# Two half-token weight units behind each of the second block's norms, in a two-block transformer kernel on one core

## The reference

```
def second_block(x, c, ...):
    x = layer_norm_2(x, emb_ln_g, emb_ln_b)
    ...
        h = x * (1.0 + sc1) + sh1
        p = h @ w_in[l]
        y_a = gmlp_spatial_gating(p[..., :MIX_A], p[..., MIX_A:2 * MIX_A], ...)
        y_b = rwkv7_time_mix(p[..., 2 * MIX_A:], ...)
        mix = jnp.concatenate([y_a, y_b], axis=-1) @ w_out[l]
        x = layer_norm_2(ALPHA * x + gt1 * mix, ln1_g[l], ln1_b[l])
        h = x * (1.0 + sc2) + sh2
        gu = h @ w_ffn_in[l]
        f = (jax.nn.silu(gu[..., :FFN_HIDDEN]) * gu[..., FFN_HIDDEN:]) @ w_ffn_out[l]
        x = layer_norm_2(ALPHA * x + gt2 * f, ln2_g[l], ln2_b[l])
```

## Time and profile before

| what | value |
|---|---|
| median of 3 executions | 1663.46 us (1661.16 to 1664.08) |
| the profiled execution's own time | 1662.28 us |
| its span in the profile | 1660.5 us |
| PE busy | 1576.3 us, 95% of the span |
| DVE, ACT, POOL busy | 995.2, 722.5, 190.9 us |
| mean granted clock of TensorE | 0.988 of full |

### The profile page before, as it was taken

The page is one execution under the profiler, slowest core; times in us unless marked ns, Lnnn a source line. Parts: engine busy times, 40 slices in busy tenths (PEclk is TensorE's granted clock), DMA queues, the critical chain, the costliest instruction groups (busy, mean ns, idle before and its releaser), DMA issues. The chain is left out here.

```text
span 1660.5 us, 24142 instructions
## 1 busy us (share of the span) xinstructions
PE 1576.3 (95%) x9852; PEld 1254.0 (76%) x9852; DVE 995.2 (60%) x1676; ACT 722.5 (44%) x1159; POOL 190.9 (11%) x159
## 2 busy tenths in 40 slices
PE   6999999999999999899999898988998999999997
PEld 5877776788788767676788687767766887888886
DVE  4999985556555476657444647776547353334445
ACT  6543367245523476557622535554424322223112
POOL 2443465400010000000005000000000000000000
PEclk9999999999999999999999999999998999999999
DMA  5232243654464322232334232200012332323331
GB/s 208 93 97 77 78 152 103 204 155 138 136 191 154 114 90 89 67 99 77 114 102 135 70 115 76 77 28 4 4 39 66 113 115 89 101 91 100 90 100 51
DMA packets 45645, 166.07 MB, mean 100 GB/s; under 512 B 5264, under 2 KB 5392, under 8 KB 45536
## 3 DMA queue, kind: packets, MB, share of 16 engines
q1 hardware_dynamic: 42912, 155.95, 29.6%
q0 software_dynamic: 2624, 8.59, 1.8%
HBM read 162.42 MB, written 2.10 MB: 99 GB/s over the span
## 5 line engine op out<-in xcount | busy, mean ns | idle before, releaser
L569 PE MATMUL bank<-h_T_hi,weight_hi 128*128 128x512 f32 x1208 | 488.2, 404 | 8.4 <-DVE conv_in L2102 3.2
L604 ACT ACTIVATE weight_hi<-raw 128x1024 fp32r<-128x1024 f32 x241 | 254.7, 1057 | 549.4 <-PE bank L571 541.0
L612 DVE TENSOR_TENSOR weight_lo<-raw,weight_hi 128x1024 fp32r<-128x1024 f32 x184 | 225.6, 1226 | 432.6 <-ACT weight_hi L604 432.6
L571 PE MATMUL bank<-h_T_hi,weight_lo 128*128 128x512 f32 x1208 | 477.2, 395 | 0.0
L570 PE MATMUL bank<-h_T_lo,weight_hi 128*128 128x512 f32 x1208 | 476.5, 394 | 0.0
L569 PEld LDWEIGHTS bank<-h_T_hi,weight_hi 128*128 128x128 f32 x1208 | 229.5, 190 | 65.8 <-issue 9.9
L570 PEld LDWEIGHTS bank<-h_T_lo,weight_hi 128*128 128x128 f32 x1208 | 229.3, 190 | 51.7 <-issue 3.9
L571 PEld LDWEIGHTS bank<-h_T_hi,weight_lo 128*128 128x128 f32 x1208 | 228.7, 189 | 50.0
L2105 DVE SCALAR_TENSOR_TENSOR bank<-conv_in,columns,bank 128x512 f32<-128x512 f32 x240 | 181.4, 756 | 8.3
L612 POOL TENSOR_TENSOR weight_lo<-raw,weight_hi 128x1024 fp32r<-128x1024 f32 x57 | 139.5, 2448 | 182.6 <-ACT weight_hi L604 182.6
L570 PE MATMUL bank<-branch_lo,weight_hi 128*128 128x512 f32 x192 | 75.5, 393 | 0.0
(11 more groups left out here) (448 smaller groups left out, 2266.5 us busy)
## 6 DMA issues: line engine op xcount, KB each, us to landing
raw<-in_weights SPq DMA_DIRECT2D x289, 512.0 KB, 3.5
x_in<-in_x SPq DMA_DIRECT2D x4, 512.0 KB, 5.5
x_rows<-in_x POOLq DMA_DIRECT2D x4, 512.0 KB, 4.9
out<-x_rows SPq DMA_DIRECT2D x4, 512.0 KB, 2.6
mem_in<-in_mem POOLq DMA_DIRECT2D x2, 512.0 KB, 8.0
ln_rows<-in_ln_g POOLq DMA_DIRECT2D x4, 256.0 KB, 4.1
ln_rows<-in_ln_b POOLq DMA_DIRECT2D x4, 256.0 KB, 4.7
silu_row<-in_c POOLq DMA_DIRECT2D x1, 512.0 KB, 11.1
```

The source lines that it names most:

```text
L569: pe.matmul(o, lhs[0], rhs[0], start=start, stop=False)
L571: return pe.matmul(o, lhs[1], rhs[0], start=False, stop=stop)
L604: act.activation(parts[n % SPLIT][0][:, :], raw[u % RAW][:, :], ACT.Copy).then_inc(*weight_hi.up(u))
L612: engine.tensor_tensor(lo[:, :], raw[u % RAW][:, :], view(hi[:, :]), ALU.subtract).then_inc(*ready.up(u))
```

## The change

The four units ("pu", 0), ("pu", 1), ("ffn_g", 0) and ("ffn_u", 0), called `EARLY`, leave the ring of three places and get hi and lo places of their own: two in the region of y_T, which the end of the first block frees, two in a region of the rwkv stage's work tiles. ACT and DVE split them behind the last unit of w_out (or w_out_2), ahead of the first row's statistics. The units that follow them take their turn in the ring of three: one is split on ACT behind the sixth piece of group 0, two behind all pieces of group 1; DVE makes all three lo parts behind all pieces.

On PE the two units run together, and in halves of the tokens: group 0's tokens with features 0 to 3 of both units, then the transposes of group 1, then group 0's tokens with features 4 to 7, then group 1's tokens with all eight. So 96 matmuls of 128x256 stand for 48 of 128x512 at each of the two places, and both results are ready at the end.

```diff
+EARLY = (("pu", 0), ("pu", 1), ("ffn_g", 0), ("ffn_u", 0))
...
-    turn_of = {u: n for n, u in enumerate(weights_of)}
+    in_turn = [u for u in weights_of if plan[u][0] not in EARLY]
+    turn_of = {u: n for n, u in enumerate(in_turn)}
...
+    here, there = Map(nc, Y_AT, H_AT), Map(nc, B_AT, M_AT)
+    early_parts = {label: (here if n < 2 else there).pair(f"early_weight{n}", [P, UNIT]) for n, label in enumerate(EARLY)}
...
-            if n >= SPLIT:
-                act.wait_ge(*given_back(weights_of[n - SPLIT]))
-            act.activation(parts[n % SPLIT][0][:, :], raw[u % RAW][:, :], ACT.Copy).then_inc(*weight_hi.up(u))
+            if plan[u][0] == EARLY[0]:
+                act.wait_ge(*y_lo.at(KT - 1))
+            elif plan[u][0] == EARLY[2]:
+                act.wait_ge(*yb_lo.at(FW - 1))
+            elif plan[u][0] not in EARLY and turn_of[u] >= SPLIT:
+                act.wait_ge(*given_back(in_turn[turn_of[u] - SPLIT]))
+            act.activation(weight_parts(u)[0][:, :], raw[u % RAW][:, :], ACT.Copy).then_inc(*weight_hi.up(u))
...
+    def first_units(pe, what, labels, rhs):
+
+
+        use = [(unit_bank(pe, label), weight_parts(index[label])) for label in labels]
+        for label in labels:
+            pe.wait_ge(*lo_ready(index[label]))
+
+        def products(g, features):
+            tokens = turned_columns(g)
+            for k in features:
+                pe.wait_ge(*turned_lo.at(what, g, k))
+                for label, (bank, (hi, lo)) in zip(labels, use):
+                    done = mm3(pe, bank[:, tokens], (hi[:, cut(k)], lo[:, cut(k)]), (rhs[0][:, k, tokens], rhs[1][:, k, tokens]),
+                               k == 0, k == KT - 1)
+                    if g and k == KT - 1:
+                        done.then_inc(*product.up(*label))
+
+        products(0, range(KT // 2))
+        pe_turn_group(pe, what, x_rows, 1)
+        products(0, range(KT // 2, KT))
+        products(1, range(KT))
+
...
     def pe_second_in(pe):
-        pe_turn_group(pe, "emb", x_rows, 1)
-        for n in range(4):
-            feature_unit(pe, ("pu", n), unit_bank(pe, ("pu", n)), h2_T,
-                         ready=(lambda k: turned_lo.at("emb", 1, k)) if n == 0 else None)
+        first_units(pe, "emb", EARLY[0:2], h2_T)
+        for n in range(2, 4):
+            feature_unit(pe, ("pu", n), unit_bank(pe, ("pu", n)), h2_T)
...
     def act_first_out(act):
         act_y_hi(act, KT - 1)
-        feed_hi(act, KT - SPLIT)
+        feed_hi(act, KT - SPLIT + 2)
...
             if t == 2:
                 act_modulated(act, what, hi, n, 0, range(6))
+                feed_hi(act)
         act_modulated(act, what, hi, n, 0, range(6, KT))
-        feed_hi(act)
-        act_modulated(act, what, hi, n, 1, range(KT // 2 + 1))
-        feed_hi(act)
-        act_modulated(act, what, hi, n, 1, range(KT // 2 + 1, KT))
-        feed_hi(act)
+        act_modulated(act, what, hi, n, 1, range(KT))
+        feed_hi(act, 2)
...
-        feed_lo(dve, KT // 2 - SPLIT)
+        feed_lo(dve, KT // 2 - SPLIT + 2)
         dve_rows(dve, "emb", h2_T, lambda t: residual(t, 1))
```

More of the change, by code:

```diff
@@ L592, in given_back, with weight_parts @@
         return product.at(*label)
+    def weight_parts(u):
+        return early_parts[plan[u][0]] if plan[u][0] in EARLY else parts[turn_of[u] % SPLIT]
     def feed_hi(act, count=1):
@@ L609, in split_lo @@
     def split_lo(engine, u, ready):
-        hi, lo = parts[turn_of[u] % SPLIT]
+        hi, lo = weight_parts(u)
         engine.wait_ge(*weight_hi.at(u))
@@ L1455, in pe_ffn @@
     def pe_ffn(pe):
-        pe_turn_group(pe, "ln1", x_rows, 1)
-        for n in range(FT):
+        first_units(pe, "ln1", EARLY[2:4], h3_T)
+        for n in range(1, FT):
             if n == 10:
                 pe_gate_rows(pe, 5)
-            feature_unit(pe, ("ffn_g", n), unit_bank(pe, ("ffn_g", n)), h3_T,
-                         ready=(lambda k: turned_lo.at("ln1", 1, k)) if n == 0 else None)
+            feature_unit(pe, ("ffn_g", n), unit_bank(pe, ("ffn_g", n)), h3_T)
             feature_unit(pe, ("ffn_u", n), unit_bank(pe, ("ffn_u", n)), h3_T)
@@ L1926, in act_second_in @@
         for n in range(4):
-            feed_hi(act)
+            if n >= 2:
+                feed_hi(act)
             act_take(act, ("pu", n), u_T[:, n, :], ACT.Gelu_apprx_tanh)
@@ L2072, in act_second_out @@
     def act_second_out(act):
-        feed_hi(act, KT - SPLIT - len(OUT_FEEDS))
+        feed_hi(act, KT - SPLIT - len(OUT_FEEDS) + 2)
     def last_spots(t):
@@ L2082, in act_ffn @@
         for n in range(FT):
-            feed_hi(act)
+            if n:
+                feed_hi(act)
             gate = act_ring.take(act, ("ffn", n), hidden_lo, n)
             act_take(act, ("ffn_g", n), gate, ACT.Silu)
-            feed_hi(act)
+            if n:
+                feed_hi(act)
             act.wait_ge(*taken["dve"].at("ffn_u", n))
@@ L2537, in dve_rows @@
             dve_modulated(dve, what, pair, 0, k)
-        feed_lo(dve)
         for k in range(KT):
             dve_modulated(dve, what, pair, 1, k)
-            if k in (KT // 2, KT - 1):
-                feed_lo(dve)
+        feed_lo(dve, 3)
     def dve_gain_rows(dve, what, t, half, gains):
@@ L2553, in dve_second_in @@
         for n in range(4):
-            feed_lo(dve)
+            if n >= 2:
+                feed_lo(dve)
             for half in range(2):
```

## The result

| | before | changed |
|---|---|---|
| median, executions beside each other | 1663.77 us (1661.16 to 1664.38, 4) | 1652.90 us (1652.38 to 1653.91, 4) |
| the same text once more (e11 below) | 1663.03 us (17) | 1654.58 us (6) |
| the profiled execution, its span | 1662.28, 1660.5 us | 1653.91, 1652.2 us |

The ratio is 0.9936 with a 95% interval of 0.9922 to 0.9950, and 0.9954 (0.9940 to 0.9968) in the repeat: 8.5 to 10.9 us by the medians, 8.4 between the two profiled executions. The prediction was 1655.3 us, faster, with a range of 1652.0 to 1659.4.

What follows compares the result with a forecast made beforehand. PE was taken as the bound, busy 95% of the span, so gains come only where it waits or runs slow. Behind emb -5.0 and behind ln1 -3.1 make -8.1 us: 1654.2 profiled, 1655.3 as a median, range 1652.0 to 1659.4.

Steps and rivals of the forecast that it cites:

- Likeliest case: PE's clock holds behind emb and falls behind ln1: together -8.1 us, a median of 1655.3; chance 0.40.
- the three cases: Clock falls behind ln1 only (1655.3 us, chance 0.40), at both places (1657.1, 0.32), at neither (1653.2, 0.13); all faster.
- Behind emb: -5.0 predicted: Third unit at 945.2 instead of 950.25: 0.5 earlier start, 2.4 less work behind transposes, 2.1 of slow clock gone.
- Two splits ahead cost 1.25: Two lo parts on DVE, 2.45 us against 1.21 idle, make residuals and last norm 1.25 us later at each place.
- 24 halves in the gap cost nothing: At each place, 24 half-width matmuls (2.9 us) run while PE stood still, done before the transposes can start.
- Halves at 0.119 and 0.22: Half-width matmuls of 128x256 on PE take 0.119 us each at full clock, 0.22 at the lower clock.
- Pieces lead PE by 2 us, third unit by 1.3: Behind emb, group 1's pieces are ready some 2 us before PE wants them, the next unit's lo part 1.3 us before.
- Behind ln1: -3.1 predicted: Third unit at 1291.6 instead of 1294.65, with 4.5 us of halves at the lower clock.
- at neither place: Rival: the clock falls neither behind emb nor ln1; ln1 gives -5.2, together -10.2, median 1653.2; chance 0.13.
- The clock's 2.1 us behind emb: Slow spell in the units behind emb disappears because the clock holds, worth 2.1 of that place's 5.0 us.
- Nothing bound the units anew: Rival: late group 1 pieces, the next lo part or a later wait eat the gain; 1660 to 1664 us, chance 0.09.
- The slower case: Rival: halves with own weight loads do not bring the clock back, all 72 at 0.239 us; 1670.6 us, chance 0.04.

Runs made afterwards that it cites:

- e11: The changed kernel run again with no edit: median 1654.58 us, ratio to the kernel before 0.9954.
- e5: The changed kernel with the lo parts of all four early units made by POOL instead of DVE: median 1654.38 us, ratio to before 0.9948.
- e10: The changed kernel with POOL making the early lo parts behind emb only, plus unread matmuls filling the gap at both places: 1652.71 us, ratio to before 0.9940.
- e3: The changed kernel with all 96 halves behind the transposes of group 1, none ahead of them: 1660.34 us, ratio to before 0.9985.
- e2: The kernel before with the change made behind ln1 alone, emb left as it was: 1657.39 us, ratio to before 0.9965.
- e1: The kernel before with the change made behind emb alone, ln1 left as it was: 1657.44 us, ratio to before 0.9965.
- e9: The kernel before with unread matmuls in the gap and again between the last transposes and first unit, both places: 1661.14 us, ratio 0.9991.
- e4: The kernel before with unread matmuls filling the gap ahead of the transposes at both places: 1660.84 us, ratio 0.9986.
- e8: The changed kernel with all early lo parts on POOL and unread matmuls filling the gap at both places: 1653.13 us, ratio to before 0.9935.
- e6: The changed kernel with one early unit at each place instead of two: 1657.32 us, ratio to before 0.9966.

## Why the prediction was right, point by point

- **Verdict and sum.** Predicted -8.1 us against the profiled execution and a median of 1655.3; the profiled execution gave -8.4, a second one -7.9, and the medians 1652.9 and 1654.6. Likeliest case (the clock holds behind emb and falls behind ln1) and place of each gain were those forecast. The chances written for the verdict are 0.01 too high for faster: the three cases and all of the unnamed make 0.87, not 0.88.
- **Behind emb: -5.0 predicted, -5.00 measured** (38.47 to 33.47). Its parts were a little off and cancelled: the start 0.84 us earlier against the lo part instead of 0.5 (before 25.60, now 24.76), the rest 4.16 instead of 4.5. That the sum came out to the hundredth is luck. The slow spell was also priced 0.2 us too high: 950.25 is where the last matmul of the second unit ends, but the third unit starts at 950.04, so the spell had cost (950.04 - 937.17) - 10.99 = 1.88 us, not 2.1.
- **Two splits ahead cost 1.25: it was 0.96 to 0.98.** I subtracted 1.21 us of idle time from the durations, 2.45. But DVE starts such instructions 1.14 us apart, so that two take 2.27 (912.22 to 914.49), and the free time between starts was 3.04 - 1.14 - 0.61 = 1.29 (residual behind lo part before, the lo part itself, the statistics between them). Tile 3's matmuls were late by 0.76 us (what follows them on PE starts 17.94 us behind the lo part, before 17.18) instead of 1.0.
- **The splits' lateness was hidden at PE, not free.** e5 and e10 behind emb show its whole 0.96 us in the end: all of it lay on the path.
- **24 halves in the gap cost nothing: right,** and they are the largest piece of the gain: 24 x 0.119 = 2.86 us of the 3.74 between e3 and the changed kernel.
- **Halves at 0.119 and 0.22: right,** 0.119 and 0.213. The price of weight loads of their own was not larger than in the cross scores.
- **Pieces lead PE by 2 us, third unit by 1.3: right, with more room;** no wait in either row, and the third unit's lo part was begun at 941.38 and done 1.23 us later, 1.9 before PE wanted it at 944.55.
- **Behind ln1: -3.1 predicted, -4.0 measured, -4.7 in e11.** This is the term that was mis-sized: a slow spell of 4.5 us in the halves was assumed, taken over from the earlier trace rows, and there were 2.1 us of it, and none in e11. The spell isn't a constant of the place; where it falls and how long it lasts in product matmuls differs between executions of one text. That it fell at all in the profile after was no certainty either: with the same order e2 shows the case that the prediction called "at neither place", and its price for ln1, -5.2, was right (-5.31).
- **What the clock was foretold from: not tested by the result.** The prediction left open whether transposes count for the clock. Behind emb it held over 3.84 us from the last early half to the next (932.00 to 935.84), as it did in e1, e5 and e11; but 3.85 us with nothing on PE had already passed at full clock before, so this doesn't decide it. And the length of the stretch did not order the cases behind ln1: 5.4 us passed in e2, and the clock fell within 2.4 us in e11.
- **The clock's 2.1 us behind emb: right in the sum, wrong as a reason by itself.** I put 2.1 us of the 5.0 down to the slow spell that would go. e9 takes away the spell alone and gets 0.45; its first unit starts no earlier than before (25.61 us behind the lo part, 25.60). The spell is worth its time only when the pieces of group 1 no longer bound the first unit, which the other parts of the change see to: no weight split among them, and eight features of group 0 to be done first. The two are not additive, and the sum came out only because both were done.
- **What was not foreseen: a spell that got longer behind.** At the wait in the rwkv stage (L1203 before, L1239 after) the clock falls in all kernels. The idle time and what follows, before and then changed:

```profile
1028.80:1033.16 4.36, 0.02 (x3) 0.03 (x1) 4.33 (x7) 3.55 (x6) 0.00 (x0) 1.00 0.38 120
1033.16:1036.50 3.34, 3.34 (x6) 2.02 (x7) 3.27 (x5) 0.00 (x0) 0.00 (x0) 0.51 0.47 157
```

```profile
1022.90:1027.57 4.67, 0.13 (x3) 0.03 (x1) 4.63 (x8) 3.86 (x6) 0.00 (x0) 0.83 0.39 112
1027.57:1032.80 5.23, 5.23 (x10) 3.45 (x11) 4.57 (x7) 1.14 (x1) 0.00 (x0) 0.50 0.31 100
```

  The wait is much the same (4.34 and 4.54 us), but PE then works slow for 5.23 us instead of 3.34, some 0.9 us lost. The mean clock over the 25 us around it is 0.93 in the four profiles without early units behind emb (before, e2, e4, e9) and 0.86 in eight of the nine with them, 0.93 in e8. So it goes with the change in these profiles; why is not shown: the work up to there is the same from the third unit on (83.12 us from it to the end of the wait before, 83.02 now), and no run here took that wait apart. Between the two places the changed kernel's profile loses 1.16 us in all (305.24 instead of 304.08), was 0.49 ahead before emb, and this makes 8.3 in the span of 9.0 at the two places. e11 has the same long spell and yet takes 303.61 us between the places. It lacks a second slow spell further on, which the changed kernel's profile has (granted clock 0.66 over 1141 to 1146, PE busy all through) and that of before too (0.66 over 1104 to 1109). Such a spell weighs as much, so one profile doesn't price the longer one in the total.
- **The rivals.** The clock did not fall behind emb in any profile with a quarter of two early units ahead of the transposes; in e3, with nothing ahead, and in e6, with a quarter of one, it did. Nothing bound the units anew. The slower case fell with the pace of the halves.

## What to carry to other kernels

Where an engine stands still ahead of a wait and then starts at a lower clock, moving real work into the standstill pays twice, but price the two apart: first ask what bounds the work behind at full clock, since a slow engine hides whatever feeds it. Splitting the consumer by tokens, so that the half that is ready runs while the other is still being normalized, was worth more here than any filling (9.0 us at the two places, against 0.7 and 1.2 for e4 and e9), and it pays to clear the feeding engine's queue of other work between the pieces. And before handing such work to POOL, look at what DVE does meanwhile: here one that reads two SBUF operands stood still until POOL's was done.

## What the runs showed of the hardware

- The granted clock can fall while PE is already dense again: in e4 at about 937.8, some 0.6 us into the first unit, behind 1.56 us of idle time and transposes with waits; with that hole filled as well (e9) it did not fall.
- With one order of instructions the slow spell behind ln1 was 2.1 us of halves, none of them, or not there, between three profiles (changed, e11, e2). The clock stood at 1.00 over 5.4 us without a product matmul in e2 and fell 2.4 us behind the last one in e11; a term of 1 to 2 us that hangs on the clock can't be told from one execution.
- POOL's two lo parts took 4.85 us behind emb and 5.67 behind ln1, where the first began beside a DVE split of two SBUF operands; DVE does both in 2.35.
